# A mixture-of-experts encoder layer: routing on the unnormalised x2, softmax block by block, selection from three sorted lists

## The reference, cut to what matters

```python
def _rmsnorm(x, g):
    x32 = x.astype(jnp.float32)
    y = x32 * lax.rsqrt(jnp.mean(x32 * x32, axis=-1, keepdims=True) + EPS)
    return (y * g.astype(jnp.float32)).astype(x.dtype)
...
    x = x + jnp.einsum('bse,ed->bsd', mixed, w_out)      # "x2" in the kernel
    h2 = _rmsnorm(x, norm2_g)
    return x + _expert_choice_moe(h2, router_w, exp_w_gate, exp_w_up, exp_w_down)
...
def _expert_choice_moe(h, router_w, w_gate, w_up, w_down):
    ...                                                  # cap = 2 * 512 // 16 = 64 tokens of each group
    affinity = jax.nn.softmax(jnp.einsum('td,de->te', xt, router_w).astype(jnp.float32), axis=-1)
    gate_vals, tok_idx = lax.top_k(affinity.T, cap)
    xs = jnp.take(xt, tok_idx, axis=0)
    hid = jax.nn.silu(jnp.einsum('ecd,edf->ecf', xs, w_gate)) * jnp.einsum('ecd,edf->ecf', xs, w_up)
    ys = jnp.einsum('ecf,efd->ecd', hid, w_down) * gate_vals[..., None].astype(h.dtype)
    out = jnp.zeros((T, D), h.dtype).at[tok_idx.reshape(-1)].add(ys.reshape(-1, D))
```

## Time and profile before

| | us |
|---|---|
| median of 3 runs | 1068.62 |
| lowest, highest | 1067.71, 1068.73 |
| the profiled execution, own time | 1069.13 |
| its span from first to last instruction | 1067.3 |
| last projection done, VectorE starts the last x2 | 447.20 (from the span's start) |
| the routing has its affinities in one place | 462.27 |
| first product of the first expert starts | 490.50 |
| mean granted TensorE clock | 0.97 of full |

### The profile page before, as it was taken

The page is one execution under the profiler, slowest core; times in us unless marked ns, Lnnn a source line. Parts: engine busy times, 40 slices in busy tenths (PEclk is TensorE's granted clock), DMA queues, the critical chain, the costliest instruction groups (busy, mean ns, idle before and its releaser), DMA issues.

```text
span 1067.3 us, 14955 instructions
## 1 busy us (share of the span) xinstructions
PE 986.8 (92%) x5031; PEld 828.8 (78%) x5031; DVE 805.8 (75%) x1005; ACT 712.2 (67%) x942; POOL 325.3 (30%) x172
## 2 busy tenths in 40 slices
PE   5999999977999999916999999999999999999995
PEld 5997998856777788815788888888888888888874
DVE  5659898787776322273889888988898889988883
ACT  5457788565796311133879777987788778877772
POOL 1000000132496000051065336633564346513320
PEclk9999999989999999957999999999999999999998
DMA  8010101000201743395999999999999999999851
GB/s 289 27 44 23 54 16 39 1 1 35 85 1 62 257 156 112 140 358 161 354 380 403 381 392 387 405 380 390 390 406 378 385 392 400 391 379 371 307 169 28
DMA packets 75248, 248.96 MB, mean 233 GB/s; under 512 B 9372, under 2 KB 16584, under 8 KB 75208
## 3 DMA queue, kind: packets, MB, share of 16 engines
q1 hardware_dynamic: 70600, 231.64, 56.8%
q0 software_dynamic: 4608, 16.78, 6.2%
HBM read 231.63 MB, written 16.78 MB: 233 GB/s over the span
## 4 chain that ended last, share of the span: by engine, by line
PE 81%; DVE 8%; ACT 5%; issue 3%; POOL 1%; DMA 1%; ACTq 0%; SPq 0%; POOLq 0%; DVEq 0%
PE bank L939 24%; PE bank L941 24%; PE bank L940 24%; PE bank L945 6%; DVE e_lo L1471 2%; ACT e_hi L870 2%; PE bank L1111 1%; PE bank L1075 1%; PE bank L1074 1%; DVE row_stat L1397 1%; PE bank L974 1%; DMA x_nat<-in_x_prompt_dram 1%; DVE top_idx L1456 1%; DVE probT_lo L1409 1%; ACT prob L830 1%
## 5 line engine op out<-in xcount | busy, mean ns | idle before, releaser
L939 PE MATMUL bank<-e_hi,xsT_hi 128*128 128x512 f32 x512 | 202.0, 394 | 1.6 <-DVE xsT_lo L1476 1.4
L941 PE MATMUL bank<-e_hi,xsT_lo 128*128 128x512 f32 x512 | 200.1, 391 | 0.0
L940 PE MATMUL bank<-e_lo,xsT_hi 128*128 128x512 f32 x512 | 199.9, 390 | 0.0
L638 POOL COPY idx_now<-idx_all 128x1 uint32 (+1 forms) x16 | 157.0, 9812 | 27.5 <-DMA y_dram<-ys,idx_now 27.5
L870 ACT ACTIVATE e_hi<-raw_gate 128x1024 fp32r<-128x1024 f32 x128 | 134.6, 1061 | 35.8 <-PE bank L941 34.2
L1471 DVE TENSOR_TENSOR e_lo<-raw_down,e_hi 128x1024 fp32r<-128x1024 f32 x128 | 146.9, 1220 | 2.4 <-ACT e_hi L870 1.5
L1471 DVE TENSOR_TENSOR e_lo<-raw_up,e_hi 128x1024 fp32r<-128x1024 f32 x128 | 146.8, 1220 | 1.4 <-ACT e_hi L870 1.3
L1471 DVE TENSOR_TENSOR e_lo<-raw_gate,e_hi 128x1024 fp32r<-128x1024 f32 x122 | 141.2, 1219 | 4.9 <-ACT e_hi L870 4.9
L870 ACT ACTIVATE e_hi<-raw_up 128x1024 fp32r<-128x1024 f32 x128 | 126.5, 1056 | 1.3 <-PE bank L941 0.3
L870 ACT ACTIVATE e_hi<-raw_down 128x1024 fp32r<-128x1024 f32 x128 | 125.1, 1059 | 1.3 <-PE bank L941 1.2
L939 PEld LDWEIGHTS bank<-e_hi,xsT_hi 128*128 128x128 f32 x512 | 96.6, 189 | 22.3 <-DVE xsT_lo L1476 1.8
(11 more groups left out here) (229 smaller groups left out, 2149.9 us busy)
## 6 DMA issues: line engine op xcount, KB each, us to landing
raw_gate<-in_exp_w_gate_dram SPq DMA_DIRECT2D x64, 1024.0 KB, 10.4
raw_up<-in_exp_w_up_dram SPq DMA_DIRECT2D x64, 1024.0 KB, 8.0
raw_down<-in_exp_w_down_dram SPq DMA_DIRECT2D x64, 1024.0 KB, 6.7
w_raw<-in_w_in_dram SPq DMA_DIRECT2D x6, 1024.0 KB, 5.3
wo_raw<-in_w_out_dram SPq DMA_DIRECT2D x8, 512.0 KB, 4.2
y_dram<-x SPq DMA_DIRECT2D x8, 512.0 KB, 5.1
h_rows<-h SPq DMA_DIRECT2D x8, 512.0 KB, 3.6
x_nat<-in_x_prompt_dram SPq DMA_DIRECT2D x4, 512.0 KB, 7.7
```

What stands on the lines that cost most here:

```text
L638: pool.tensor_copy(idx_now[:, 2:3], idx_all[:, bass.ds(e, 1)] if not isinstance(e, int) else idx_all[:, e:e + 1]).then_inc(idx_copied, 1)
L939: pe.matmul(out, l_hi, r_hi, start=first, stop=False)
L940: pe.matmul(out, l_hi, r_lo, start=False, stop=False)
L941: return pe.matmul(out, l_lo, r_hi, start=False, stop=last)
```

## The change

The router works on x2 as it is: g2 is multiplied once into the router's weights (GpSimd), and 1/root of each row comes in as the scale of the exponential. So the turning and the logits of a block no longer wait for its norm. TensorE's list is woven anew: the turning of block b-1 stands after k = 1 of block b, its logits after k = 3, and all of it is inside the projection. Softmax is done for each block (`soft_shift`, the exponential on ScalarE with the sum from its accumulator, `soft_share`), its 16 columns are turned at once (`turn_aff`), and the selection begins as soon as a list is complete. There are three lists: group 0 (512 columns), blocks 4 and 5 (256), blocks 6 and 7 (256). Each takes 8 rounds of finding the eight largest and replacing them, on 16 partitions; round r works in the partition quarter r mod 4, so one search for positions over 112 partitions serves four rounds. The two lists of group 1 are merged at the end: one sorted down against the other reversed, the larger of each pair is kept. h2 is now made by ScalarE (x2 times rstd) and GpSimd (times g2). Beside it: the first four gathers take their indices straight from `idx_all`; the first product waits for the first half of the low parts only; VectorE takes over rows 3 to 5 of the first six low parts (POOL_ROWS = 3); three down pieces (before: two) are issued only after the gather has landed, and all four gate pieces of expert 1 behind it.

```diff
+    SPLIT, POOL_ROWS = 6, 3
...
+        pool.tensor_tensor(router[:, :, :], router[:, :, :], vecs[:, V_G2:V_G2 + KC].unsqueeze(2).to_broadcast([P, KC, E]),
+                           ALU.mult).then_inc(router_done, 1)
+        for b in range(NB):
+            pool.wait_ge(h2_scaled, b + 1)
+            pool.tensor_tensor(h2[:, b % 2, :], h2[:, b % 2, :], g2b[:, :], ALU.mult).then_inc(h2_done, 1)
         pool.wait_ge(outproj_done, NB)
-        for j in range(SPLIT):
+        for j in range(POOL_ROWS):
...
-            pool.tensor_copy(idx_now[:, p:p + 1], idx_all[:, e:e + 1]).then_inc(idx_copied, 1)
-            pool.wait_ge(idx_copied, e + 1)
...
+            act.activation(root1[:, b:b + 1], sumsq1[:, b:b + 1], ACT.Sqrt, scale=1.0 / D, bias=eps).then_inc(root2_done, 1)
...
+            if b < NB - 1:
+                scale_h2(b)
+            act.activation(small[:, 124 + b:125 + b], eps, ACT.Exp)
...
+            act.activation(aff_e[:, b, :], bank[:, 7, b * E:(b + 1) * E], ACT.Exp, scale=rstd1[:, b:b + 1], bias=aff_stat[:, 1, b:b + 1],
+                           accum_out=aff_stat[:, 2, b:b + 1]).then_inc(aff_exp_done, 1)
+            if b == NB - 1:
+                scale_h2(b)
+            else:
+                act.activation(small[:, 132 + b:133 + b], eps, ACT.Sqrt)
...
+            for k in range(0 if b else WO_EARLY, KC):
+                ins = project_out(b, k)
+                if b and k == 1:
+                    turn_x2(b - 1)
+                    if b >= 2:
+                        turn_aff(b - 2)
+                if b and k == 3:
+                    logits_of(b - 1)
+            ins.then_inc(outproj_done, 1)
+        turn_x2(NB - 1)
+        turn_aff(NB - 2)
+        logits_of(NB - 1)
+        turn_aff(NB - 1)
...
-        pe.wait_ge(xsT_lo_done, 2)
+        pe.wait_ge(xsT_lo_done, 1)
...
+        def top_round(n, r):
+            f, rows, cols = r // QUADS, quad_of(n, r), list_cols(n)
+            eight = slice(8 * f, 8 * f + 8)
+            dve.max(top_val[rows, n, eight], work[rows, f, cols]).then_inc(top_done, 1)
+            dve.wait_ge(top_done, ROUNDS * n + r + 1)
+            if r < ROUNDS - 1:
+                link(dve.match_replace(work[quad_of(n, r + 1), (r + 1) // QUADS, cols], top_val[rows, n, eight], work[rows, f, cols], -1.0))
+        def find(n, f):
+            used, eight = 32 * (QUADS - 1) + E, slice(8 * f, 8 * f + 8)
+            dve.max_index(top_idx[0:used, n, eight], top_val[0:used, n, eight], work[0:used, f, list_cols(n)]).then_inc(found, 1)
...
+        for b in range(NB):
+            x2_block(b)
+            if b == NB - 1:
+                top_round(1, ROUNDS - 1)
+                find(1, 0)
+                dve.wait_ge(x2T_done, 2 * b + 1)
+                dve.wait_ge(logits_done, b - 1)
+                dve.tensor_copy(x2T[:, b % 2, 0:4, :], bank[:, 4, :].rearrange("p (k t) -> p k t", k=4)).then_inc(x2T_out_v, 1)
+                find(1, 1)
+            rstd2(b)
...
+        affinities(2, NB - 1, NB)
+        for r in range(ROUNDS):
+            top_round(2, r)
+        compare()
+        find(2, 0)
+        find(2, 1)
+        stack_second()
```

More of the change, by code:

```diff
@@ L903, in _ @@
             hi_row(0, 0, raw_gate, gate_loaded, 16, j)
+        act.wait_ge(best_done, 1)
+        for q in range(QUADS):
+            ins = act.activation(stacked[:, 1, CAP + 16 * q:CAP + 16 * q + 16], merge[32 * q:32 * q + E, 4, :], ACT.Copy)
+        ins.then_inc(vals_stacked, 1)
         turn_hi(xsT_hi[:, 0, :, :], xsT_done, 0, xsT_hi_done)
```

304 lines of the change are left out of this document (182 added, 122 removed).

## The result

| | before | changed |
|---|---|---|
| median, us | 1068.65 | 1057.90 |
| lowest, highest of four | 1067.71, 1068.73 | 1057.22, 1061.32 |
| profiled execution | 1069.13 | 1058.12 |
| its span | 1067.3 | 1056.2 |

The ratio of the times is 0.9903, with a 95% interval of 0.9891 to 0.9915: 10.7 us less. I had said 1056.5, within 1053.5 to 1062.

What follows compares the result with a forecast made beforehand. TensorE was taken as the bound (81% of the chain), not leading for 43.3 us from last x2 to first product. Steps A to F summed to -12.2 us, giving 1056.5; range 1053.5 to 1062, at 0.85.

Steps and rivals of the forecast that it cites:

- A: First to last x2: TensorE work moved ahead of the last x2 adds 5.6 us, bounds 4.8 to 6.5.
- E: Turning of gathered tokens to first product: starting after half the split saves 0.85 us, bounds 0 and -0.9.
- C: Selection, from list complete to lists turned: shorter rounds plus a merge save 8.4 us, bounds -7.3 to -9.0.
- D: Gather after routing: without the index copy it starts sooner, -1.0 us, between 0 and -1.1.
- B: Last x2 to list complete: -7.6 us; -6.8 with a 2.66 table switch; bounds -5.8 (half-clock logits) and -8.0.
- rival 3: Selection rounds: replacing into another partition quarter is dear, eating the gain from 0.91 us extra; mild or rival 4: 0.05.
- F: Kernel beginning: one more 4 KB transfer (g2) and 52 columns instead of 44, +0.1 us, 0 to 0.4.
- What is late next: Before `routed` and during the gather: GpSimd, h2 store and VectorE rows are covered by 1.8, 2.7 and 0.9 us.
- rival 1: Routing tail keeps part of the gain, as with earlier half clock (1.8 us): 1059 to 1061; 0.22 with Rival 2.
- Rival 2: Routing: GpSimd's way or the h2 store becomes last, costing 1 to 3 us: 1057.5 to 1059.5; 0.22 with rival 1.
- rival 4: Expert phase: later weight refill makes ScalarE wait, up to 5 us: 1061; 0.05 together with a mild rival 3.
- First product to the end: Expert phase, from the first product to the kernel's end: claimed unchanged at 576.8 us.

## Why the prediction held, step by step

The time was 1.4 above the forecast and inside the range (1.9 by all twelve runs). Part of that closeness is luck. Steps A to E brought 9.6 us in the traces where the sum had 12.25 for them (C 1.7 and D 1.0 less). The stretch ahead of the first x2 and the one behind the first product brought another 1.5, which the change did not earn: both are places where the clock falls sooner or later from run to run. What went otherwise, in the order of the steps:

- **A** was right: +5.88 for 5.6. TensorE has no gap in the blocks, as the cover worked out for VectorE said, and there would have been cover for h2 too (96.19 with it).
- **B** was right: -7.86 for -7.6. The table load was hidden: 455.65 to 456.93, and the exponential at 457.79 waited for VectorE. The load with its first use kept ScalarE until 457.14, so the 2.66 us that the Trainium skill (ScalarE: Activation LUTs, What ACT_TABLE_LOAD costs) gives for a switch, on which I had put -6.8, isn't seen here. The logits ran at half clock, the condition of the bound of -5.8, in six of the thirteen profiles since. That cost 0.9 to 1.45 us and not the 1.8 reckoned, so B is -6.4 at the least.
- **C** was mis-sized: -6.66 for -8.4, outside its bounds. The rounds are 0.42 and 0.41, and a replacement into another quarter costs at most 0.01 more, so rival 3 is gone. The failed term is "four small operations of the merge (0.75)". The first of them was held 1.6 us by GpSimd's row, a wait that the prediction put at nothing; without the hold, selection takes 10.10, the 10.0 of the working.
- **D** failed: 0 for -1.0. The gap of 0.94 behind the index copy is the gather's own issue and stayed as 1.03. The gather started 0.15 us sooner behind `routed` (1.18 before, 1.03) and the turning came 0.15 later behind its start (4.58, 4.73). The lower bound of 0 had allowed for it; I took the wrong end, since no row told the two apart.
- **E** was right to the hundredth as a stretch, 3.35 to 2.50; how much of it reaches the end is not shown.
- **F** costs nothing measurable; the 0.7 us between the first two traces there were chance.
- **What is late next**: nothing was. GpSimd's rows ended 3.1 us ahead of `routed`; the h2 store had landed by 468.50 (t = 16.25 for 15.5). The margin was right and the wrong question: GpSimd's rows were in time for their reader and still in the way of a neighbour.
- **Rivals 1, 2 and 4**: the refill made no wait. Before, the clock fell at 453.3 rather than 453.5, by the 0.66 of its window. The half clock of rival 1 is real, but its onset comes sooner or later between runs of one kernel. Rival 2, that the way through GpSimd becomes the last, named the engine but not the mechanism.
- **First product to the end**: 576.14 for 576.8, by two chances of opposite sign. Here the first hidden layer came 28.71 us after the first product (27.77 before), since the clock came back only 5.7 us after it (3.8 before), and the last expert had no stretch at half clock (26.20 and not 27.87 from the last hidden layer to the end).

## What to carry over

Before work moves to an idle engine, ask not only whether it finishes in time but which operations of its neighbours it runs beside: a VectorE operation with two SBUF inputs may stand still for the rest of GpSimd's instruction, and a small GpSimd operation for the rest of VectorE's. Keep long GpSimd rows out of the stretch in which VectorE's short operations are the path, or put one-input operations there. Look for such a hold in the trace of before: an operation of one form that once takes longer than its twins, while the other engine is at work. Where TensorE idles ahead of a long phase, turnings that nobody reads, each group released by the progress of the others, gave back 1.5 to 2.7 us up to the first hidden layer; but count them, since 32 at once delayed the work that they serve by 1.0.

## What the runs showed of the chip that I had not expected

- The hold lasts to the end of the running instruction, whatever the size of the one held: 0.73, 1.80 and 2.38 us for operations that take 0.16 to 0.18 alone, 1.13 for a copy of one column that took 0.19. MAX8, MATCH_REPLACE8 and FIND_INDEX8 at 0.41 to 0.42 beside GpSimd were not held. Nor were two-input operations of which one input lies in PSUM: in the changed kernel's trace eight `probT_lo<-bank,probT_hi` run wholly inside a two-input operation of GpSimd, and take 0.67 to 0.69 like the other 56.
- The clock's changes move between runs of one kernel, and in the three profiles of the changed kernel they make up the spread. They have four places here: 1.5 us in the attention stage, 0.9 to 1.45 in the last logits, up to 1.2 in the first expert (27.5 to 28.7 us to the first hidden layer), 1.6 in the last one (26.2 or 27.8). The Trainium skill (TensorE: Matmul & The Clock Gate, Part 1) says that one kernel can show different counts of slow matmuls from run to run; the traces agree. For a change of 1 us here, stretches read from the trace decide and medians don't.
- The clock comes back with dummy work as well. In the first of the two kernels with extra turnings it was at half from 457.0; TensorE had done almost nothing but such turnings since 462.21 when it was granted in full again at 467.2 (mean 0.89 in the window 467 to 468). In both, the matmuls of the first expert all ran at full clock, where in the profiles without extra turnings the first 3.2 to 5.7 us did not.
